# First mixing stage of a three-block transformer kernel: engine orders rewritten, taps moved between engines, first products by halves of the input channels

## The reference

```python
h = rms_norm(x, norm1_g[l])
proj = h @ w_in[l]
q, k, v, u = jnp.split(proj, [ATTN_WIDTH, 2 * ATTN_WIDTH, 3 * ATTN_WIDTH], axis=-1)
q = apply_rope(rms_norm(q, q_norm_g[l]), cos, sin)
k = apply_rope(rms_norm(k, k_norm_g[l]), cos, sin)
attn = moba_attention(q, k, v)            # here: causal, 8 heads of 64
conv = conformer_conv(u, ...)             # GLU, causal depthwise conv of 31 taps, layer norm, silu
x = x + jnp.concatenate([attn, conv], axis=-1) @ w_out[l]
```

## Time and profile before

| | us |
|---|---|
| median of 3 runs | 1353.07 (1352.94 to 1353.79) |
| profiled execution | 1353.88 |
| its span, first to last instruction | 1351.8 |
| around the span | 2.1 |

### The profile page before, as it was taken

One profiled execution on the slowest core, in us unless ns is written; L12 is line 12 of the kernel. 1 busy time (PEld: TensorE's weight loads), 2 busy tenths in 40 slices (PEclk: granted clock), 3 DMA queues, 4 the chain that ended last, 5 costly groups with the idle time before them and its releaser, 6 DMA issues.

```text
span 1351.8 us, 19356 instructions
## 1 busy us (share of the span) xinstructions
PE 1318.7 (98%) x7626; PEld 1156.7 (86%) x7626; DVE 825.5 (61%) x989; ACT 680.8 (50%) x910; POOL 137.4 (10%) x162
## 2 busy tenths in 40 slices
PE   8988999999999999999999999999999999999998
PEld 7976888888888889998888888888888999888886
DVE  6985665555665547668766555665556544665553
ACT  5675454443544435455555443554444655554441
POOL 3552000000000000312000000000000441000000
PEclk9998999999999999999999999999999999999999
DMA  8423565555655554224475555565554853465540
GB/s 274 144 98 103 202 218 187 187 195 165 206 199 185 194 183 136 83 94 156 153 261 196 191 195 186 171 213 195 192 195 129 265 150 107 168 218 187 186 155 32
DMA packets 174354, 235.02 MB, mean 174 GB/s; under 512 B 5375, under 2 KB 154127, under 8 KB 174288
## 3 DMA queue, kind: packets, MB, share of 16 engines
q1 hardware_dynamic: 170368, 223.52, 49.0%
q0 software_dynamic: 3184, 9.37, 2.2%
q10 hardware_dynamic: 736, 1.19, 0.2%
HBM read 233.03 MB, written 1.05 MB: 173 GB/s over the span
## 4 chain that ended last, share of the span: by engine, by line
PE 88%; DVE 7%; ACT 3%; issue 1%; POOL 1%; DMA 0%; DVEq 0%; ACTq 0%; POOLq 0%
PE psum L1097 22%; PE psum L1049 16%; PE psum L1051 16%; PE psum L1050 16%; PE psum L1101 11%; DVE w_lo L1646 2%; PE psum L1278 1%; PE psum L1286 1%; PE psum L1173 1%; DVE psum L1882 1%; DVE ws L1710 1%; ACT ws L455 1%; PE psum L1277 1%; PE psum L1296 1%; PE psum L1295 1%
## 5 line engine op out<-in xcount | busy, mean ns | idle before, releaser
L1646 DVE TENSOR_TENSOR w_lo<-raw,w_hi 128x2048 fp32r<-128x2048 f32 (+1 forms) x212 | 482.8, 2282 | 96.7 <-ACT w_hi L436 95.6
L436 ACT ACTIVATE w_hi<-raw 128x2048 fp32r<-128x2048 f32 (+1 forms) x212 | 401.7, 1902 | 31.8 <-PE psum L1051 9.7
L1097 PE MATMUL psum<-t_both,w_hi 128*128 128x512 f32 x1280 | 327.5, 393 | 0.0
L1097 PEld LDWEIGHTS psum<-t_both,w_hi 128*128 128x128 f32 x1280 | 230.2, 189 | 41.0
L1049 PE MATMUL psum<-w_hi,t_both 128*128 128x256 f32 (+2 forms) x712 | 233.7, 328 | 4.6 <-DVE t_both L1992 1.5
L1051 PE MATMUL psum<-w_hi,t_both 128*128 128x256 f32 (+2 forms) x712 | 229.0, 322 | 0.0
L1050 PE MATMUL psum<-w_lo,t_both 128*128 128x256 f32 (+2 forms) x712 | 228.9, 321 | 0.0
L1049 PE MATMUL psum<-w_hi,f_hi 128*128 128x512 f32 x488 | 193.2, 396 | 1.3 <-issue 1.3
L1051 PE MATMUL psum<-w_hi,f_lo 128*128 128x512 f32 x488 | 190.9, 391 | 0.0
L1050 PE MATMUL psum<-w_lo,f_hi 128*128 128x512 f32 x488 | 190.7, 391 | 0.0
L1101 PEld LDWEIGHTS psum<-t_both,w_lo 128*128 128x128 f32 x1280 | 174.6, 190 | 12.3
(11 more groups left out here) (178 smaller groups left out, 1289.2 us busy)
## 6 DMA issues: line engine op xcount, KB each, us to landing
raw<-in_ffn_wg SPq DMA_DIRECT2D x44, 1024.0 KB, 5.5
raw<-in_ffn_wu SPq DMA_DIRECT2D x44, 1024.0 KB, 5.2
raw<-in_ffn_wd SPq DMA_DIRECT2D x44, 1024.0 KB, 4.9
raw<-in_even_w_in SPq DMA_DIRECT2D x13, 1024.0 KB, 5.0
raw<-in_odd_w_in SPq DMA_DIRECT2D x12, 1024.0 KB, 5.3
raw<-in_w_gate SPq DMA_DIRECT2D x11, 1024.0 KB, 5.5
raw<-in_w_up SPq DMA_DIRECT2D x11, 1024.0 KB, 5.3
raw<-in_w_down SPq DMA_DIRECT2D x11, 1024.0 KB, 4.9
```

Source lines behind the costliest of these rows:

```text
L436: nc.scalar.activation(w_hi[:, n % SLOTS, 0:w], raw[:, n % RAWS, 0:w], ACT.Copy).then_inc(hi_done, 1)
L1097: mm = nc.tensor.matmul(o[:, :], wh[:, k, cs], t_both[:, k, :, :].rearrange("p a s -> p (a s)"), start=k == 0, stop=k == KT - 1)
L1646: nc.vector.tensor_tensor(w_lo[:, n % SLOTS, 0:w], raw[:, n % RAWS, 0:w], w_hi[:, n % SLOTS, 0:w].bitcast(F32), ALU.subtract).then_inc(lo_ ...
```

## The change

On TensorE, the first unit's products are ordered by halves of the input channels (new `by_channels_first`); the heads begin one after another in steps 7 to 14; the convolution has five pieces, three for tile 3 and two for taps 25 to 30 of tile 2, in steps 11 to 15; the products of `rows(0, 0)` stand behind the loop, and `rows(1, 1)` goes ahead of groups 2 and 3. On VectorE, the input edge is written out of its own (`input_edge`): the second mean square ahead of half of the first tile's products, low parts of both tiles for the first half of the channels, then for the second. In the mix it does six taps fewer, at other places, adds the side sum for two channel tiles at once, and has the splits of units 11 to 13 behind the mean. On ScalarE and GpSimd the same operations stand in another order, with the splits of units 11 to 13 behind the heads. The branches for the input in `edge_x` go.

```diff
-        PIECES = [(tap, min(tap + 4, TAPS)) for tap in range(PE_FROM, TAPS, 4)]
+        ACT_CT, ACT_PE, DVE_PE = 1, 3, 2
+        SINGLES = 11
+        PE_TAPS = {ACT_PE: range(20, TAPS), DVE_PE: range(25, TAPS)}
+        PIECES = [(ct, tap, min(tap + 4, TAPS)) for ct in (ACT_PE, DVE_PE) for tap in range(PE_TAPS[ct].start, TAPS, 4)]
         DVE_TAPS = ([(tap, 0) for tap in range(11)]
                     + [(tap + 11 * (ct == 0), ct) for tap in range(TAPS - 11) for ct in (2, 0)]
-                    + [(tap, 2) for tap in range(TAPS - 11, TAPS)])
+                    + [(tap, 2) for tap in range(TAPS - 11, PE_TAPS[DVE_PE].start)])
 
         block = stack.enter_context(nc.Block())
 
...
                 keep_rope(units[6][3], 7)
-                taps(2)
                 keep_pt(L, 0)
                 exps(L, 1)
-                taps(1)
-                split_to(12)
+                taps(2)
+                square(8)
                 keep_pt(L, 1)
                 exps(L, 2)
-                square(8)
-                taps(2)
+                taps(3)
                 keep_pt(L, 2)
                 exps(L, 3)
-                taps(1)
-                split_to(13)
-                keep_pt(L, 3)
+                taps(2)
                 keep_rope(units[8][3], 7)
                 keep_unit(ph, 9)
+                taps(1)
+                keep_pt(L, 3)
+                exps(L, 4)
                 taps(2)
-                exps(L, 4)
                 keep_pt(L, 4)
-                taps(2)
-                split_to(14)
                 exps(L, 5)
                 group_hi(0, 6)
                 keep_pt(L, 5)
-                taps(2)
                 exps(L, 6)
                 keep_pt(L, 6)
                 exps(L, 7)
                 keep_pt(L, 7)
+                split_to(12)
+                group_hi(1, 7)
+                split_to(13)
                 act.wait_ge(cen_ok, 1)
...
-                group_hi(1, 7)
+                split_to(14)
                 for g in range(2):
                     act.wait_ge(z_ok, g + 1)
                     for ct in range(2 * g, 2 * g + 2):
...
                     root(0)
-                    add(2)
+                    add(3)
                     root(1)
                     add(3)
                     root(2)
-                    add(6)
+                    add(7)
                     root(3)
-                    add(3)
+                    add(5)
                     build(1)
-                    add(6)
+                    add(2)
+                    build(2)
...
+            def by_channels_first(b):
+
+                wh, wl = w_cols(0)
+                for half in range(2):
+                    pe.wait_ge(lo_done if half else half_lo, 1)
+                    pe.wait_ge(t_lo_ok, 2 * half + 2)
+                    for c in range(2):
+                        for k in range(4 * half, 4 * half + 4):
+                            mm = three(bank[b][:, c * S:(c + 1) * S], wh[:, k, c * P:(c + 1) * P], wl[:, k, c * P:(c + 1) * P],
+                                       t_hi[:, k, :], t_lo[:, k, :], k == 0 and c == 0, k == KT - 1 and c == 1)
                 mm.then_inc(unit_used, 1)
...
                 tile_ready(1, 0)
-                tile_ready(1, 4)
-                for j in range(4):
+                by_channels_first(ph["bank"][0])
+                by_channels(n0 + 1, ph["bank"][1])
...
+                    ct, lo, hi = PIECES[p]
...
                 turned_after = {4: 4, 6: 5, 8: 6, 11: 8}
-                begun = {7: 0, 8: 1, 9: 2, 10: 3, 12: 4, 13: 5, 14: 6, 15: 7}
-                piece = {12: 0, 13: 1, 14: 2}
                 for i in range(16):
                     if i < 12:
                         tile(4 + i // 2, i % 2)
-                    if i == 15:
-                        pe.wait_ge(bank_free[0], left[8])
-                        pe.wait_ge(bank_free[1], left[9])
-                        rows(0, 0, (0,))
-                    if i in piece:
-                        conv(piece[i])
                     if i in turned_after:
                         turned(turned_after[i])
-                    if i == 14:
+                    if i >= 11:
+                        conv(i - 11)
+                    if i == 13:
                         group_turn(V["o"][0], 6)
-                    if i in begun:
-                        scores(begun[i])
-                    if i - 1 in begun:
-                        turn(begun[i - 1])
-                    if i - 2 in begun:
-                        values(begun[i - 2])
-                turn(7)
-                values(6)
+                    if 7 <= i < 15:
+                        scores(i - 7)
+                    if 8 <= i:
+                        turn(i - 8)
+                    if 9 <= i:
+                        values(i - 9)
+                pe.wait_ge(bank_free[0], left[8])
+                pe.wait_ge(bank_free[1], left[9])
+                rows(0, 0, (0,))
+                values(7)
                 rows(0, 0, (1,))
+                group_turn(V["o"][1], 7)
                 pe.wait_ge(conv_ok, 2)
...
-                values(7)
-                rows(0, 1, (0,))
-                group_turn(V["o"][1], 7)
+                rows(0, 1)
                 pe.wait_ge(sq4_ok, 1)
                 for t in range(T):
...
-                rows(0, 1, (1,))
+                rows(1, 0, (0,))
                 pe.wait_ge(rstd_ready, ph["rstd"])
                 for t in range(T):
                     mm = nc.tensor.matmul(bank[5][:, t * P:(t + 1) * P], st[:, 10 + t:11 + t].broadcast_to([P, P]), ident[:, :],
                                           start=True, stop=True)
                 mm.then_inc(spread_ok, 1)
-                rows(1, 0)
+                rows(1, 0, (1,))
+                rows(1, 1)
                 rows(2, 0)
                 rows(3, 0)
-                rows(1, 1)
                 rows(2, 1)
                 rows(3, 1, (0,))
                 turn_x(ph["next"], 0)
...
+                mean_square(0)
+                dve.wait_ge(g_spread, 2)
+                dve.wait_ge(rstd_ready, nx(rstd_ready))
+                normed(0, 0)
+                dve.wait_ge(x_in[1], 16)
+                mean_square(1)
+                normed(0, 1)
+                dve.wait_ge(rstd_ready, nx(rstd_ready))
+                normed(1, 0)
+                normed(1, 1)
+                dve.wait_ge(half_hi, 1)
+                h = slice(0, UNIT // 2)
+                nc.vector.tensor_tensor(w_lo[:, 0, h], raw[:, 0, h], w_hi[:, 0, h].bitcast(F32), ALU.subtract).then_inc(half_lo, 1)
+                for half in range(2):
+                    for t in range(T):
+                        turned(t, half)
+                nx(t_hi_ok, 4)
+
             def edge(ph):
                 if ph["take"] == "input":
-                    edge_x(ph, 0)
-                    edge_x(ph, 1)
-                    dve.wait_ge(half_hi, 1)
-                    h = slice(0, UNIT // 2)
-                    nc.vector.tensor_tensor(w_lo[:, 0, h], raw[:, 0, h], w_hi[:, 0, h].bitcast(F32), ALU.subtract).then_inc(half_lo, 1)
-                    edge_turned(ph, 0)
-                    edge_turned(ph, 1)
...
-                taps(4)
+                taps(7)
                 split_to(6)
-                taps(3)
                 glu(3)
-                taps(6)
+                taps(5)
                 split_to(7)
...
                 mean_square(2)
                 rope_begin(6)
+                split_to(9)
+                maxima(L, 0)
+                rope_end(6)
+                taps(5)
+                maxima(L, 1)
+                split_to(10)
+                taps(3)
+                maxima(L, 2)
                 taps(2)
-                rope_end(6)
-                taps(4)
-                maxima(L, 0)
-                split_to(10)
-                maxima(L, 1)
-                taps(4)
-                maxima(L, 2)
                 mean_square(3)
                 rope_begin(8)
                 taps(2)
+                maxima(L, 3)
                 rope_end(8)
-                maxima(L, 3)
-                taps(4)
                 split_to(11)
                 taps(4)
+                maxima(L, 4)
+                taps(6)
+                maxima(L, 5)
                 group_out(L, 0, V["o"][0], 6)
-                split_to(12)
-                maxima(L, 4)
-                taps(5)
-                maxima(L, 5)
+                taps(2)
+                maxima(L, 6)
                 group_lo(0, 6)
                 taps(4)
-                maxima(L, 6)
-                split_to(13)
-                taps(3)
                 maxima(L, 7)
                 taps(TAPS)
+                group_out(L, 1, V["o"][1], 7)
+                dve.wait_ge(conv_ok, 2)
                 dve.wait_ge(piece_done, len(PIECES))
                 dve.wait_ge(tap_added, TAPS - 1)
-                nc.vector.tensor_tensor(V["acc"][:, PE_CT, :], bank[3][:, 0:S], V["acc"][:, PE_CT, :], ALU.add).then_inc(side_ok, 1)
```

(7 more changed lines are left out.)

59 lines of the change are left out of this document (32 added, 27 removed).

## The result

| | us |
|---|---|
| changed kernel, median of 4 runs | 1340.96 (1339.3 to 1343.3) |
| kernel before, 4 runs beside it | 1353.01 (1352.2 to 1353.8) |
| ratio | 0.9906, 95% interval 0.9894 to 0.9918 |
| profiled execution, its span | 1340.76, 1338.7 |
| forecast, range | 1340.1, 1335.5 to 1346 |

A forecast was written before the change was run, and what follows sets the result against it. TensorE, busy 98% of the span, was taken as the bound; -1.3 -14.1 -5.0 +2.8 +0.5 +2.4 +1.7 gave about -13.0 us, from 1353.88 profiled to 1340.9, or 1340.1 us for the median; range 1335.5 to 1346.

The forecast's parts named there:

- The start (-1.3): Input edge: first product moves from 14.28 to about 13.0 us, after the third low part, and the shift is carried.
- Rival (d): Input edge: reordered beginning brings nothing because the second tile's transposes set it; +1.3, 1341.4 us; chance 0.05.
- Idle behind the start (-14.1, with +0.5 and +2.4 as new waits): First mix: TensorE's 14.1 us of idle go; new waits at third rotary step (0.5) and next edge (2.4).
- Three slow stretches (-5.0): First mix: three stretches of about 3.4 us at 1.2 GHz after waits go, 1.7 us each, 5.0 us together.
- The added products (+2.8): Convolution on TensorE: six more taps cost 2.8 us, all on the path.
- The end of the mix (+2.4): Before next edge's transposes: unit 15's load follows unit 12's split, so TensorE waits 2.4 us, bounded by 0 and 4.
- The slow stretch behind it (+1.7): Behind the wait before the next edge: one slow-clock stretch booked, 1.7 us, bounds 0 and 1.7.
- GpSimd beside VectorE (taken as 0): Diagonals for convolution pieces 3 and 4: an addition meeting a VectorE split costs TensorE 0 to 1.2 us, taken as 0.
- (b): End of mix: all works, last wait draws no slow clock or loads land early enough to halve it; 1337.8 us; chance 0.22.
- (c): Heads: small operations through ScalarE and GpSimd stay the bound, 0.6 us per head, +4.8; 1344.9 us; chance 0.17.
- (e): First feed-forward pair: weights come late and it also waits, +7, 1347 us; chance 0.05.
- (f): GpSimd and VectorE shared access: twelve additions stretched by 1.34 us add 16 us; slower than before, 1356 us; chance 0.03.

The follow-up runs named there:

- old beginning: Changed kernel with the old order of VectorE's input edge, low parts and first unit's products, against the changed kernel; 1341.73 us.
- narrow additions: Changed kernel with GpSimd's tap additions cut to 8 of 256 columns, leaving convolution sums incomplete, against the changed kernel; 1337.69 us.
- late split of unit 15: Changed kernel with VectorE's low part of unit 15 made after the next edge's first tile is normalised; single execution 1336.37 us.
- the same, timed: Changed kernel with unit 15's low part after the next edge's first tile, timed over six runs; 1337.23 us, ratio 0.9878 to the kernel before.
- late split, two low parts: Changed kernel with unit 15's low part after the next edge's first tile and no wait for the third low part; 1337.90 us, ratio 0.9883.
- all three edits: Changed kernel without the third low part's wait, unit 12 split before the scaling, unit 15's low part after the next edge's first tile; 1338.70 us, ratio 0.9888.
- the change again: The changed kernel run once more with nothing edited, for the spread; 1341.03 us, ratio 0.9902.

## Why the prediction was right, point by point

**The start (-1.3).** Right in place, size and reason: 14.28 to 13.02, after the third low part. What I did not foresee is its condition. It seems to be carried in the new order (0.9 us of 1.4 against the mean of five executions, from one execution of the old beginning), returns nothing in the old order, and a further 0.6 us was worth nothing in the one execution that tried it alone. Rival (d), in which the start brings nothing, came true in the kernel before, though for another reason: the queues behind it, not the second tile's transposes. There is also a piece beside the sum: the clock rose 5.1 us after the first product before, and 3.9 us after it now. The stretch of the changed kernel up to the rise:

```profile
13.02:17.00 3.98, 3.98 (x18) 3.98 (x19) 3.17 (x3) 2.34 (x4) 1.12 (x3) 1.00 1.11 239
```

and of the kernel before:

```profile
14.28:19.40 5.12, 5.12 (x24) 5.12 (x25) 3.86 (x3) 3.96 (x3) 0.00 (x0) 1.00 1.01 313
```

Products of 256 columns came every 0.21 to 0.22 us in both (3.98 / 18; 5.12 / 24), twice the spacing that follows (44 in the next 5.00 us of either kernel, 0.11). The granted clock printed there has no record for the first microseconds; the spacing has to be read. With 1.14 us less at half pace some 0.6 us is won. It is not the change's doing: executions of the same beginning have 1 to 18 products at half pace. Nor does it decide much here, since the two executions of the change, with 18 and 1, have the mean at the same place.

**Idle behind the start (-14.1, with +0.5 and +2.4 as new waits).** Right: 14.1 us of waits have become 3.5 (2.48 at the end, 0.6 for rotary parts, 0.4 of issue), so -10.6 against a forecast of -11.2. The third rotary step's wait came as 0.34 us for the turned unit, and the first maxima at 63.49 (forecast 63). The largest single cause is shown: the splits among the heads, by the run that put them back.

**Three slow stretches (-5.0).** Right: all three are gone in both executions. The run with the splits put back has two again, each behind a wait of 1.8 to 2.0 us. That the clock falls because of such waits is likely by their order, and not tested by itself.

**The added products (+2.8).** Right, and the run without them shows that they cost nothing in the end. What they save (3.3 us of waits among the heads) had no term of its own in my working; it was part of the idle that was to go.

**The end of the mix (+2.4).** The chain worked out was that of the trace, link by link, in the changed kernel (SyncE's load, ScalarE, then VectorE):

```profile
114.57 0.37 SPq L388 DMA_DIRECT2D raw<-in_w_up  x1
...
119.79 1.92 ACT L437 ACTIVATE w_hi<-raw 128x2048 fp32r<-128x2048 f32 x1 [2.79 <-DMA raw<-in_w_up]
...
121.74 2.29 DVE L1649 TENSOR_TENSOR w_lo<-raw,w_hi 128x2048 fp32r<-128x2048 f32 x1 [1.42 <-ACT w_hi L437]
123.95 1.28 DVE L1678 TENSOR_TENSOR x_sb<-psum,x_sb 128x512 f32<-128x512 f32 x2
```

From the load's issue, T = 114.57, it is 13.26 us to the transposes, where T + 13.3 was worked out, and the wait was 2.48. The match in size is partly luck: the load's 5.2 us was 6.0 in the second execution (wait 3.32) and 6.5 in the run with six taps on VectorE (wait 3.75). Moving the addition ahead of that split removes the wait.

**The slow stretch behind it (+1.7).** Not in the first profile of the change, in the second it was. The step was right as one of two outcomes, and should have been booked as such. That the median still came within 1 us of the forecast owes to the additional stretch between 508 and 526.

**GpSimd beside VectorE (taken as 0).** This step failed. The diagonals were the wrong place to look: they were built by 92.94, the piece that needs them began at 93.13, and TensorE did not wait. The cost lies in VectorE, in the chain that feeds the rotary steps: the last operation of such a step takes 1.67 us for 0.69, a split next to additions up to 3.39 us for 2.28, and that costs TensorE up to 3.1 us, as the run with narrow additions shows. The sum did not suffer, probably because the kernel before has the same 19 additions (31.5 us there, 31.2 now), and its rotary operation took 1.66 us too: the price stood in both. No run leaves the additions out of the kernel before, so this is argued. I had looked at the lengthened GpSimd operation and not for the lengthened VectorE one. The Trainium skill, page SBUF — State Buffer, section "SBUF: two separate sides", says that whichever of the two starts first holds the port pair for its whole instruction and the other is blocked; the split of 3.38 us (behind a GpSimd addition) and the power of 2.68 us (behind a split) are its two directions, and both agree.

**The rivals.** (a) gave the time. (b) held in one point, in one profile: no slow clock behind the wait. (c) fell: TensorE waits for no exponential among the heads. (e) fell: the feed-forward pair lost no more than 0.8 us, and that in the late-split version. (f) had the right mechanism, but up to 3.1 us of it and not 16, on VectorE's side, and hardly as something new.

**What stays open.** Why executions of one kernel differ in the pace of their first products, in the landing of unit 15 and in the clock later on. And whether the cost of the additions can be saved without leaving them out: no run moved them.

## What to carry to other kernels

Where one engine bounds the program, lay its partners' queues beside it and move their long operations (here weight splits of 2 us) out of the stretch in which short ones are waited for, to a place where the bounding engine has a queue of its own work; then extra work on the bounding engine can pay too, if it stands where it would wait. Take the terms of such a sum as conditional: an earlier start was worth about 1 us in the new order and nothing in the old. Before a difference of 1 us at some place is given to an edit, look how far the same program moves there from one execution to the next, and measure from the last place at which the two programs are still the same. And where two engines share a port, look for the lengthened operation on both sides, the tiny one too: two elements per partition waited out a 2.28 us split.

## What the hardware showed beyond expectation

The time of one program varies with the number of stretches of about 3.3 us at 1.2 GHz. In six of the profiled executions, without those at the start and in the last 4 us:

| kernel | stretches | us |
|---|---|---|
| late split of unit 15 | 0 | 1336.37 |
| the same, timed | 1 | 1336.61 |
| late split, two low parts | 1 | 1337.90 |
| all three edits | 2 | 1339.55 |
| the change | 2 | 1340.76 |
| the change again | 3 | 1342.03 |

Each costs about half its length, some 1.7 us. The stretches of the second model's mix do not follow a wait. Each begins within 1 us of the end of 24 products of only 40 columns, in which TensorE waits for nothing; in the changed kernel (first and last of the 24, and the first product at half pace):

```profile
505.40 0.18 PE L1050 MATMUL psum<-w_hi,t_both 128*128 128x40 f32 x1
...
507.89 0.27 PE L1052 MATMUL psum<-w_hi,t_both 128*128 128x40 f32 x1
...
508.69 0.41 PE L1052 MATMUL psum<-w_hi,t_both 128*128 128x256 f32 x1
```

Every one of these executions has two such groups there, 12 to 14 us apart, and the clock fell behind both, behind the second alone, or behind neither. Behind waits it is no different: the last wait of the first mix drew a slow stretch at 2.66, 3.32 and 3.75 us and none at 2.48, 2.60 and 2.68 us, and 1.4 us drew one in the kernel before. So by these rows whether the clock falls is not settled by the program alone. A difference of one or two stretches, up to 3 us here, between two kernels is read off the stretches before it is given to an edit: of the 3.7 us between the medians of the change and of the late split, 1.8 to 3.4 us are the edit's, and the rest comes with the missing stretches. The two ratios' intervals, 0.9894 to 0.9918 and 0.9861 to 0.9896, only just touch.
